# GpSimd takes the seven products of the backward keys with their block totals from VectorE (HGRN2, Conformer and MoE layer, one core)

## The reference

```python
b = jnp.cumsum(log_f, axis=3)
decay = jnp.exp(jnp.where(mask, b[..., :, None, :] - b[..., None, :, :], -jnp.inf))
scores = jnp.einsum('bnhtd,bnhtsd,bnhsd->bnhts', q, decay, k)
o_intra = jnp.einsum('bnhts,bnhse->bnhte', scores, v)
```

## Time and profile before

| | |
|---|---|
| median of 3 runs | 834.47 us (833.5 to 837.01) |
| profiled execution, its own time | 835.81 us |
| span of the profile | 834.0 us |
| TensorE busy | 793.0 us (95%) |
| VectorE busy | 381.6 us (46%) |
| ScalarE busy | 236.2 us (28%) |
| GpSimd busy | 20.9 us (3%), 22 instructions |
| granted TensorE clock | 0.989 of full, mean |

### The profile page before, as it was taken

How to read it: one execution, slowest core, us unless ns; L and a number is a source line. 1 busy time by engine, 2 the same in 40 slices (tenths; PEclk the granted TensorE clock), 3 DMA queues, 4 the chain that set the end, 5 groups by cost and what they waited for, 6 DMA issues and landing times.

```text
span 834.0 us, 12875 instructions
## 1 busy us (share of the span) xinstructions
PE 793.0 (95%) x5234; PEld 545.1 (65%) x5234; DVE 381.6 (46%) x773; ACT 236.2 (28%) x400; POOL 20.9 (3%) x22
## 2 busy tenths in 40 slices
PE   4999999999999999999999999799999999989984
PEld 2779897999999999965555455354554745445222
DVE  1176999879987755583232312212222112112114
ACT  3163747344445353231111111111111101011001
POOL 1000010100000100100000000000000000000000
PEclk9999999999999999999999999999999999999998
DMA  8998797523442479869999999999999999999995
GB/s 331 408 362 332 283 410 293 194 101 103 152 152 101 152 236 372 369 233 423 391 425 426 421 426 426 422 425 426 421 427 420 422 423 425 423 425 425 426 420 202
DMA packets 81221, 284.71 MB, mean 341 GB/s; under 512 B 5256, under 2 KB 12040, under 8 KB 64520
## 3 DMA queue, kind: packets, MB, share of 16 engines
q1 hardware_dynamic: 80664, 282.55, 85.2%
q10 hardware_dynamic: 496, 1.30, 0.4%
HBM read 280.67 MB, written 3.16 MB: 340 GB/s over the span
## 4 chain that ended last, share of the span: by engine, by line
PE 64%; SPq 18%; DMA 11%; DVE 2%; issue 2%; ACT 1%; POOL 0%; DVEq 0%; POOLq 0%
SPq L628 14%; PE bank L2112 13%; PE bank L2168 7%; PE bank L1727 6%; PE bank L1729 6%; PE bank L1732 6%; DMA chunk<-in_w_expert_down 5%; PE bank L2019 3%; PE bank L1996 3%; PE bank L1789 3%; PE bank L1713 3%; PE bank L1771 3%; DMA chunk<-in_w_expert_gate_up 2%; PE bank L1674 2%; DMA ring<-in_w_out 2%
## 5 line engine op out<-in xcount | busy, mean ns | idle before, releaser
L2112 PE MATMUL bank<-chunk,xg 128*64 128x512 f32 (+2 forms) x1024 | 196.9, 602 | 8.9 <-DMA chunk<-in_w_expert_gate_up 8.7
L2112 PEld LDWEIGHTS bank<-chunk,xg 128*64 128x64 f32 (+2 forms) x1024 | 62.2, 127 | 136.9 <-issue 121.9
L2168 PE MATMUL bank<-chunk,act_t 128*64 128x512 f32 (+2 forms) x480 | 98.2, 620 | 3.7 <-DMA chunk<-in_w_expert_down 3.6
L1526 DVE SCALAR_TENSOR_TENSOR act_r<-bank,w_slot,sil 128x256 f32<-128x256 f32 x26 | 12.6, 484 | 166.1 <-ACT sil L995 166.1
L1538 DVE TENSOR_TENSOR y_lo<-bank,y_hi 128x512 fp32r<-128x512 f32 x52 | 35.8, 691 | 76.5 <-ACT y_hi L1008 76.5
L995 ACT ACTIVATE sil<-bank 128x256 f32<-128x256 f32 x26 | 10.0, 384 | 194.7 <-PE bank L2112 194.7
L1090 DVE TENSOR_TENSOR ring_lo<-ring,ring_hi 128x1024 fp32r<-128x1024 f32 x44 | 52.9, 1219 | 23.5 <-ACT ring_hi L777 23.3
L2168 PEld LDWEIGHTS bank<-chunk,act_t 128*64 128x64 f32 (+2 forms) x480 | 30.0, 131 | 51.2 <-issue 50.3
L1008 ACT ACTIVATE y_hi<-bank 128x512 fp32r<-128x512 f32 x52 | 30.9, 597 | 104.8 <-PE bank L2168 100.4
L1150 DVE SCALAR_TENSOR_TENSOR conv<-upad,dw,conv 128x256 f32<-128x256 f32 x120 | 52.8, 512 | 0.0
L777 ACT ACTIVATE ring_hi<-ring 128x1024 fp32r<-128x1024 f32 x44 | 44.4, 1054 | 27.3 <-PE bank L1753 12.6
(11 more groups left out here) (316 smaller groups left out, 1205.6 us busy)
## 6 DMA issues: line engine op xcount, KB each, us to landing
chunk<-in_w_expert_gate_up SPq DMA_DIRECT2D x128, 1024.0 KB, 20.2
chunk<-in_w_expert_down SPq DMA_DIRECT2D x63, 1024.0 KB, 22.3
ring<-in_w_in SPq DMA_DIRECT2D x16, 2048.0 KB, 9.7
ring<-in_w_ada SPq DMA_DIRECT2D x12, 2048.0 KB, 9.8
ring<-in_w_proj_hgrn SPq DMA_DIRECT2D x2, 2048.0 KB, 7.6
ring<-in_w_out SPq DMA_DIRECT2D x2, 2048.0 KB, 14.1
ring<-in_w_proj_conv SPq DMA_DIRECT2D x1, 2048.0 KB, 7.7
chunk<-in_w_shared_gate_up SPq DMA_DIRECT2D x2, 1024.0 KB, 22.8
```

Of the source, the lines that this page charges most:

```text
L2112: ins = mm(bank[2 + b][row:row + width, :], xg[:, k, c:c + width], w[:, k % 4, :], start=(k == 0), stop=(k == KD - 1))
L2168: ins = mm(out[row:row + width, :], act_t[:, c, row:row + width], w[:, c, h * 512:(h + 1) * 512], start=(c == 0), stop=(c == 1))
```

## The change

The product of the backward keys (L1221) leaves VectorE's queue at all seven levels and enters GpSimd's queue, ahead of the convolution's `rsqrt` for levels 0 to 2 and behind it for levels 3 to 6. GpSimd's product of a level waits for the totals of the level before (tot_done), for both key products of the level before (k_done), for this level's mix_keys (mix_done) and for the first query products (q_done at 2). It doesn't wait for the level's scores. k_done is still raised twice a level, once by each engine.

```diff
@@ gpsimd
-            pool.wait_ge(cms_done, 1)
-            rsqrt(rms_c, ssq_c, 2).then_inc(crms_done, 1)
+            for level in range(LEVELS):
+                m = 1 << level
+                kb, tb = halves(qk[:, 3, :], level), halves(fg[:, 1, :], level)
+                if level:
+                    pool.wait_ge(tot_done, level)
+                    pool.wait_ge(k_done, 2 * level)
+                pool.wait_ge(mix_done, level + 1)
+                pool.wait_ge(q_done, 2)
+                nc.gpsimd.tensor_tensor(kb[:, :, 1, :], kb[:, :, 1, :], tb[:, :, 0, 0:1].broadcast_to([P, 8 * P // m, m]), ALU.mult).then_inc(k_done, 1)
+                if level == 2:
+                    pool.wait_ge(cms_done, 1)
+                    rsqrt(rms_c, ssq_c, 2).then_inc(crms_done, 1)
@@ vector, in the loop over the levels
-                kf, kb = halves(qk[:, 2, :], level), halves(qk[:, 3, :], level)
+                kf = halves(qk[:, 2, :], level)
...
-                V.tensor_tensor(kb[:, :, 1, :], kb[:, :, 1, :], tb[:, :, 0, 0:1].broadcast_to([P, nb, m]), ALU.mult).then_inc(k_done, 1)
```

## The result

| | before | after |
|---|---|---|
| median, 13 runs each | 834.87 us (833.5 to 838.58) | 838.73 us (836.42 to 841.62) |
| profiled execution, its own time | 835.81 us | 836.96 us |
| VectorE busy | 381.6 us | 379.6 us |
| GpSimd busy | 20.9 us | 36.9 us |
| granted clock | 0.989 | 0.993 |

The changed kernel takes 1.0045 times as long, 95% interval [1.0032, 1.0058]: 2.7 to 4.8 us more, 3.8 in the middle, where 3.2 (837.7 us) was forecast. The forecast called 0.5% about the least that a measurement can tell from no change; the interval here is 0.13% to either side, so this 0.45% is told from none. The profiled execution of after is one of its quickest, only 1.15 us over that of before, so I read it by stretches and not by its total.

A forecast was written before the change was run, and what follows sets the result against it. TensorE was taken to bound the levels, so VectorE's relief counted 0; stalls of 0.50 + 1.44 + 0.63 + 0.63 = 3.2 us on the median of 834.47 gave 837.7 us, range 833.6 to 841.5.

The forecast's parts named there:

- the relief at 0: In the levels, seven products leaving VectorE free 7.9 us of its queue, worth 0 us directly because TensorE runs without a gap.
- the hold: While GpSimd's product reads SBUF, VectorE instructions with two SBUF inputs stand; 2.26 us for 1024 elements.
- level 3's rsqrt: The convolution's rsqrt ahead of level 3's product begins 1.13 us earlier, takes 1.01 us and ends at about 220.6.
- Levels 0 and 6 cost nothing: Level 0: VectorE idles 3.69 us, more than a whole hold; level 6 has no splits.
- gap forecast: TensorE's stall before the second half of a level's scores: 0.50, 1.44, 0.63 and 0.63 us at levels 1, 3, 4, 5.
- if GpSimd wins: At level 3, GpSimd's product starts before VectorE's first split, which waits nearly the whole hold; 2.15 us in either order.
- Passing the stalls on in full: Each microsecond TensorE loses in the levels moves the rest of the program by one, through the copies of the final states.
- A (hidden): Rival, 20%: the hold falls elsewhere or TensorE's pace covers it; time as before, 834.5 us (to 835.5).
- B (dearer operands): Rival, 17%: strided operands cost more on GpSimd, a hold of 2.50 us or more; 838.7 to 844.1 us.
- C: Rival, 3%: VectorE's queue paces TensorE somewhere, so its relief shows; all of it would give 826.6 us.

The follow-up runs named there:

- e3: Kernel before with VectorE's product of the backward keys left out at all levels and made by nobody; levels -0.02 us, total not comparable.
- e9: Changed kernel with level 1's GpSimd product alone waiting until VectorE has copied out tiles 0 and 1; levels +1.67 us, total 838.42 us, one run.
- e2: Kernel before plus an extra GpSimd product of the backward keys by ones at the change's moments; levels +1.97 us, total 1.0029 of before.
- e4: Changed kernel with GpSimd's product replaced by a memset of all the backward keys at all levels; levels -0.02 us, total not comparable.
- e1: Changed kernel with GpSimd's product of each level waiting until VectorE has copied out tiles 0 and 1; levels -0.04 us, total 1.0013 of before.
- e6: Kernel before with the change at levels 3 to 6 only; levels +0.82 us, total 0.9999 of before.
- e7: As e2, but the extra GpSimd instruction is a one-input tensor_scalar times 1.0, 128x2048; levels +13.30 us, total 848.61 us, one run.
- e8: As e2, but the second input is 1024 moving fetches of ones, steps of 4 to 32 bytes by level; levels +3.81 us, total 841.98 us, one run.

## Why the prediction was right

**What bounds the kernel, and the relief at 0:** shown. TensorE's levels are as long without the product (e3, -0.02 us), so 7.9 us of VectorE's queue were worth nothing by themselves. Beside the hold the relief isn't nothing level by level: it causes level 3's gap (e9) and spares part of those of levels 1 and 5 (e2). The prediction counted its effect on level 3's rsqrt, and took it for nothing at levels 1 and 5, where the splits wait for ScalarE.

**The hold** of VectorE's two-input work, read from a convolution tap of 2.62 us beside the sum of keys: shown by e4, where writing alone holds nothing, and by e1, where the product stands beside PSUM-fed tiles and costs nothing. Levels 0 and 6 cost nothing, as said; level 2 too. "Two-input" was too narrow: e2's scalings on one array were held as well.

**The sizes**, where the steps were off and partly made each other good:

| level | gap forecast | gap measured | what was mis-sized |
|---|---|---|---|
| 1 | 0.50 | 1.02 | held 1.96 us, taken as 1.34: product 2.85, not 2.42, and its start 0.15 later |
| 3 | 1.44 | 0.77 | held 1.59 us, taken as 2.15: rsqrt 0.72, not 1.01, product 2.14, not 2.42 |
| 4 | 0.63 | 0.34 | held 1.14 us, taken as 1.33: product 2.04, its start 0.15 later |
| 5 | 0.63 | 0.27 | held 1.08 us, taken as 1.33: product 1.97, its start 0.15 later |
| each | | 0.1 less | tile 0 took 0.71 to 0.74 us, not 0.75, and TensorE went on 0.05 us behind it, not 0.14 |
| restarts | 0 | 0.4 | 0.1 behind each gap |

The row "each" holds for every one of the four levels: at level 1, for example, tile 0 is copied from 192.81 to 193.52 and TensorE begins at 193.58.

The term that failed is the hold of 2.26 us, one value for all levels, from the sum of keys whose two inputs both move. Its argument that VectorE's L1221 takes 1.22 us at every level was no guide for GpSimd. At level 3 the forecast said "if GpSimd wins, the first split waits for nearly the whole hold; if the split wins, the second one does", and so counted the whole hold for either order. Neither order cost that. In the change GpSimd starts 0.40 us ahead of the wanted split, and that part of its length is free. Where the split wins (e2, e6) it is the rsqrt that stands behind the first split, the product falls behind both, and TensorE loses nothing. The rsqrt's 1.01 us came from the ones on 128x4; the trace of before has one on 128x2, at 356.13, with 0.71. The sum, 3.2 us against 2.81, was nearer than its terms: level 1 came out 0.52 us dearer, levels 3 to 5 together 1.32 cheaper, and the restarts added 0.4. That the sum is so near is in part luck.

**Passing the stalls on in full:** the totals agree with it (2.81 us in the levels, 2.7 to 4.8 in the total; e2 1.97, and 1.1 to 3.8), and so does e7, one run with 13.3 and 13.3. The single runs e8 and e9 took more in total than in the levels, by 2.9 and 1.3 us, which the scatter of the stretch behind 300 us covers. Whether the 1 us between 2.81 and the middle of the interval is more than scatter isn't shown.

**Rivals:** A (hidden) is what e1 makes of the change. It fell for the change itself, since ScalarE sets the moment of the splits, and did so at all four levels, one more than the prediction counted. B (dearer operands) was real at levels 0 and 1 and reversed at levels 3 to 6; it didn't decide. C fell with e3, since relief alone gave TensorE nothing. No version measured here beats the kernel before: with the hold placed well, TensorE still paces the levels.

## What to carry to other kernels

Before work goes from VectorE to GpSimd, list what VectorE does in the next 2 to 3 us after GpSimd starts: an instruction with two SBUF inputs stood until GpSimd's product was nearly over, and so did a scaling of one SBUF array; one fed from PSUM didn't. An added wait that moves the product behind the urgent pair of splits took the whole cost away, although the product then ended later. And where the engine relieved isn't the one that paces the stage, relief is worth nothing and may shift other work into a worse moment.

## What the runs showed of the hardware that I had not expected

- A GpSimd product of 128x1024 fp32 took 1.90 to 1.93 us undisturbed when its second input was one repeated element (e2, levels 0 and 4 to 6, so with blocks of 1 to 64 in the first input), 2.38 to 2.46 us when it moved (e8), and 1.94 to 2.89 us with block totals, longest with the most different totals.
- A GpSimd tensor_scalar in place, 128x2048, took 5.37 us (2.6 ns an element), against 1.9 ns an element for the two-input product with a repeated input, and it held VectorE as well; a memset of the same size took 1.81 and held nothing.
- VectorE's scaling of 128x256 with two scalars a partition took 2.02 us beside GpSimd's product (e2) and 5.45 us beside its tensor_scalar (e7), against 0.41 alone.
- A held instruction shows no wait in the profile: its own duration grows (a split from 1.22 to 3.19 us), and the wait stands only at the engine behind it.
- The small rsqrt took 0.72 us with VectorE idle and 1.65 to 1.74 when it began together with a split.
